# A two-block transformer kernel on one core: its prologue rearranged (scale rows first, shift rows last, squares added by GpSimd)

## The chip, the cores and the metric

One core of a Trainium2 chip runs the whole program. The metric is the device time of one execution in microseconds. Engine names are those of the profile: PE is TensorE's matmul, PEld its weight load, DVE VectorE, ACT ScalarE, POOL GpSimd, SP SyncE, whose queue issues the DMAs.

## The reference, cut to what matters

Two transformer-like blocks work on 1024 tokens of 1024 features in float32. The change touches only the start of the first one, up to its first gated products:

```
m = silu(c) @ a_mod_w + a_mod_b           # c is one row; m = shift, scale, gate
h = rmsnorm(x, a_norm_g) * (1 + scale) + shift
b_gate, c_gate, u, z = split(h @ a_w_in, 4)
y = b_gate * causal_dwconv(c_gate * u, a_conv_w) * silu(z)
```

`rmsnorm` divides every token by the root of the mean of its squares. This factor is one number for a token, so that `h @ w` equals `(x * g * (1 + scale)) @ w`, multiplied by the token's factor, plus `shift @ w`. The kernel uses this for the first two products: it starts them before the sum of squares is known.

## The kernel before, in words

Activations lie transposed: a feature tile is [128 features x 1024 tokens], and X is eight such tiles (k = 0 to 7). A product of one "chunk" gives 128 output features: eight steps (one for each k), each of six matmuls of 512 columns, because every operand is split in a high and a low part (HH and HL for activations, WH and WL for weights) and three of the four cross products are kept (`mm3`, L843; `step`, L851). A chunk's result stands in a pair of PSUM banks (PAIR[0] to PAIR[3]). ACT writes the high part of the weights (WH) from the loaded row WR, and POOL the low part (WL = WR - WH, L2747), each for a 128x1024 tile. With PAIR[0] and PAIR[1] and two slots each for WH and WL, chunks normally take turns.

The prologue before the change runs as follows.

- **SP** (L558 to L577) issues the DMAs in this order: the row c, the vectors (VEC), the weights of chunks 0 and 1, the four pieces of X (two tiles, 1 MB each) with two small constants behind the first piece, then for k = 0 to 7 the shift row and the scale row of `a_mod_w` (MRAW, 512 KB each), then the weights of chunks 2, 3 and 4, each behind a wait.
- **Squares**: ACT squares the eight tiles of X into XSQ (L1455), DVE adds them in pairs (L2133), and PE sums the four pairs over the partitions with a matrix of ones (L908).
- **Modulation**: `modulation` (L2115) multiplies a row tile with silu(c) and sums along it, which gives 128 values of shift or scale; it is called a dot below. `shift_and_scale(k)` (L2138) makes two dots and two operations of one column: the shift goes to MOD, the coefficient g * (1 + scale) to COEF.
- **Raw phase**: for each k, ACT writes HH = X * COEF (L1463), DVE writes HL = X * COEF - HH (`raw_low`, L2148), and PE makes the step k of chunks 0 and 1 (`input_chunks`, L914). Ahead of each step pair PE multiplies the split weights of the two chunks with the shift column of k (four matmuls of one column, L924), which gives the term `shift @ w` of chunks 0 and 1.
- **Fill**: `root` (L1427) makes the tokens' factors on ACT (Ln, then Exp). Then for each k DVE writes X * COEF * factor (L2050), ACT adds the shift and rounds it to HH (L1438), and DVE writes the low part HL (`fill_lo`, L2066; L2084). PE makes chunks 2 and 3 with these operands (`two_chunks`, L872), chunk 3 lagging one step behind chunk 2 until five of its steps are done. At k = 2 of the fill, DVE reads the raw results of chunks 0 and 1 out of PSUM into AE (L2166). ACT makes WH of chunks 2 and 3 in the same two slots that chunks 0 and 1 used, so after these have ended.
- **After the fill**: DVE multiplies the gates, runs the convolution and the products (`input_products`, L2177), then the six dots of the next 48 modulation rows, and PE goes on with chunk 4 and the loop over j.

The order on each engine is written out by hand; semaphores with constant counts tie the engines together. The rest of the program (attention, the second block, the two feed-forward matrices) is the same in both kernels.

Of the kernel before, what the change touches and what calls it, by code (L numbers as in the profile page):

```python
# [25 lines left out]
P = 128  # L26
# [165 lines left out]
def block_kernel(nc, xt, cb, vecs, consts, mods, wst, out):  # L192
    with ExitStack() as ctx:
        def sem(name):
            return ctx.enter_context(nc.semaphore(name))
# [54 lines left out]
        XSQ = nc.alloc_sbuf_tensor_at("XSQ", [P, KT * S], F32, offset=HL_AT)  # L250
        WR1 = nc.alloc_sbuf_tensor_at("WR1", [P, D], F32, offset=HL_AT - 4 * S)
        AE = [nc.alloc_sbuf_tensor_at(f"AE{i}", [P, S], F32, offset=(SCR0 + 127) // 128 * 128 + 4 * S * (6 + i)) for i in range(2)]
        WR3 = nc.alloc_sbuf_tensor_at("WR3", [P, D], F32, offset=(SCR0 + 127) // 128 * 128 + 4 * S)
# [124 lines left out]
        def vec(name, i=0):  # L378
            return col(VEC, i + _V[name])
# [35 lines left out]
        ld_c = sem("ld_c")  # L415
        ld_cb = sem("ld_cb")
# [5 lines left out]
        sq_pair = sem("sq_pair")  # L422
# [26 lines left out]
        a_raw_read = sem("a_raw_read")  # L449
        a_shift = sem("a_shift")  # L450
# [94 lines left out]
        def _(sp):  # L545
            def load_w(c, at=None):
                sp.wait_ge(w_lo, c)
                sp.dma_start(WR0[:, :], row(wst, c if at is None else at)).then_inc(ld_w, 16)
# [11 lines left out]
            sp.dma_start(VEC[:, :], vecs).then_inc(ld_c, 16)  # L560
            sp.dma_start(WR0[:, :], wst[0]).then_inc(ld_w, 16)
            sp.dma_start(WR1[:, :], wst[1]).then_inc(ld_w1, 16)
            for g in range(4):
                sp.dma_start(X[:, 2 * g * S:2 * (g + 1) * S], xt[:, 2 * g * S:2 * (g + 1) * S]).then_inc(ld_x[g], 16)
                if g == 0:
                    sp.dma_start(IDF[:, :], consts[:, K_ID:K_ID + P]).then_inc(ld_c, 16)
                    sp.dma_start(TRF[:, :], consts[:, K_TRI:K_TRI + P]).then_inc(ld_c, 16)
# [274 lines left out]
        def _(pe):  # L842
# [62 lines left out]
            for k in range(0, KT, 2):  # L905
                pe.wait_ge(sq_pair, k // 2 + 1)
                for h in (0, HALF):
                    last = pe.matmul(PS[:, 2 * S + h:2 * S + h + HALF], ONES[:, :], kt(XSQ, k)[:, h:h + HALF],  # L908
                                     start=k == 0, stop=k == KT - 2)
                    last.then_inc(ss if h and k == KT - 2 else sq_added, 1)  # L910

            u = USED["ain"]

            def input_chunks(j, first=False):  # L914
                if first:
                    pe.wait_ge(free[0], u[0])
                    pe.wait_ge(free[1], u[1])
                    pe.wait_ge(w_hi, C_AIN + 2)
                    pe.wait_ge(w_lo, C_AIN + 2)
                    for k in range(KT):  # L920
                        pe.wait_ge(a_raw_lo, k + 1)
                        for m in range(2):
                            for half in (WH[m], WL[m]):
                                pe.matmul(PS[:, 3 * S + m * HALF:3 * S + m * HALF + 1], half[:, k * P:(k + 1) * P].bitcast(F32),  # L924
                                          col(MOD, k), start=k == 0 and half is WH[m], stop=k == KT - 1 and half is WL[m])
# [485 lines left out]
        def _(act):  # L1411
# [41 lines left out]
            for k in range(KT):  # L1453
                act.wait_ge(ld_x[k // 2], 16)
                ins = act.activation(kt(XSQ, k), kt(X, k), ACT.Square)  # L1455
                if k:
                    ins.then_inc(sq, 1)
            act.wait_ge(s_sc, 1)
            for k in range(KT):
# [4 lines left out]
                if k == 0:  # L1464
                    load_ln()
                    act.wait_ge(ss, 1)
                    root(T[0], PAIR[2], TP)

            def first_input(k):
                if k < KT - 1:  # L1470
                    act.wait_ge(a_raw_read, k + 1)
                if k == 2:
                    split_w(2, 0)
                if k == 3:
                    act.wait_ge(ld_w, 48)
                    act.wait_ge(chunk_done, 3)
                    act.activation(WH[1][:, :], WR3[:, :], ACT.Identity).then_inc(w_hi, 1)
                    for m in range(2):
                        ins = act.activation(SM[:, 12 + m:13 + m], PS[:, 3 * S + m * HALF:3 * S + m * HALF + 1], ACT.Identity)
                    ins.then_inc(a_shift, 1)  # L1480
                    act.wait_ge(a_shift, 1)
                    act.wait_ge(free[1], 2)
                    act.activation(AE[1][:, :], AE[1][:, :], ACT.Identity, bias=SM[:, 13:14]).then_inc(ain_cu, 1)

            fill_hi("a", 0, before=first_input)
            act.wait_ge(ld_c, 48)
# [6 lines left out]
            def input_gates(j, first=False):  # L1493
# [5 lines left out]
                split_w(4 * j + 4, 0)  # L1499
# [6 lines left out]
                act.activation(T[2], PAIR[1], ACT.Sigmoid).then_inc(ain_sg, 1)  # L1506
# [506 lines left out]
            unit_hi(48, 0, 0)  # L2013
            unit_hi(48, 0, 1)
# [3 lines left out]
            unit_hi(48, 0, 2)  # L2018
            unit_hi(48, 0, 3)
            for i in range(5, 7):  # L2020
                down_weights_hi(0, 0, 0, i)
            unit_hi(48, 0, 4)
            hidden(UPS - 1, 1)
            unit_hi(48, 0, 5)
            unit_hi(48, 0, 6)
# [20 lines left out]
        def _(dve):  # L2046
# [77 lines left out]
            dve.wait_ge(ld_c, 48)  # L2124
# [6 lines left out]
            for k in range(0, KT, 2):  # L2131
                dve.wait_ge(sq, k + 1)
                dve.tensor_tensor(kt(XSQ, k), kt(XSQ, k), kt(XSQ, k + 1), ALU.add).then_inc(sq_pair, 1)  # L2133

# [3 lines left out]
            def shift_and_scale(k):  # L2138

                dve.wait_ge(ld_k[k], 32)  # L2140
                for dst, m in ((col(MOD, k), k), (col(COEF, k), KT + k)):
                    modulation(dst, MRAW[:, m * D:(m + 1) * D])
                dve.wait_ge(mod_done, 2 * k + 2)
                dve.tensor_tensor(col(MOD, k), col(MOD, k), vec("mod_b", k), ALU.add)
# [10 lines left out]
            shift_and_scale(0)  # L2155
            dve.wait_ge(ss, 1)
            for k in range(1, KT):
                shift_and_scale(k)
                raw_low(k - 1)
            raw_low(KT - 1)  # L2160

            def first_input(k):
                if k == 2:
# [13 lines left out]
            def input_products(j, first=False):  # L2177
# [4 lines left out]
                if first:  # L2182
                    dve.wait_ge(a_shift, 1)
# [14 lines left out]
                dve.tensor_tensor(T[3], PAIR[0], T[3], ALU.mult).then_inc(free[0], 1)  # L2198
# [5 lines left out]
                dve.tensor_tensor(T[2], PAIR[1], T[2], ALU.mult).then_inc(free[1], 1)  # L2204
# [538 lines left out]
        def _(pool):  # L2743
# [9 lines left out]
            split_w(2, 0)  # L2753
            pool.wait_ge(w_hi, 4)
            pool.tensor_tensor(WL[1][:, :], WR3[:, :], WH[1][:, :].bitcast(F32), ALU.subtract).then_inc(w_lo, 1)
# [221 lines left out]
```

## Time and profile before

| | us |
|---|---|
| median of 3 runs | 2800.58 (2798.49 to 2803.13) |
| span of the profiled execution | 2802.3 |
| PE busy | 2707.3 (97%) |
| DVE busy | 1614.1 (58%) |
| ACT busy | 1189.8 (42%) |
| POOL busy | 1109.0 (40%) |

The time of the profiled execution is its span, 2802.3 us; no other time was recorded for it. It lies within the three runs, 1.7 us above their median.

A row of the timeline gives the start in us from the span's start, the time in us, engine and line, what was written and read, how many instructions are merged (x2), and in brackets how long the engine had been idle before, and what ended that. A row of the stretches gives the stretch, its length, then for each engine the busy time and the number of instructions. A row of the chain gives start, us and what the time is put down to. Two records are written for each matmul with float32 operands that are not split.

### The profile page before, as it was taken

The numbers are of one execution on the slowest core, as the hardware profiler recorded it, in microseconds if no ns is written. First come the engines' busy times: TensorE is split into PE (matmuls) and PEld (weight loads), VectorE is DVE, ScalarE is ACT, GpSimd is POOL, SyncE is SP. The second block draws the span as 40 slices with busy tenths as digits, with TensorE's granted clock in tenths as the row PEclk, the third lists the DMA queues.
The fourth block names the chain that finished last, engine by engine and source line by source line (L and its number), as shares of the span: only waits on it lengthen the run. The fifth ranks groups of instructions, "written<-read, shape, count | busy, mean of one in ns | idle before, by whom it ended". The sixth has DMA issues, their size and how long they took to land.

```text
span 2802.3 us, 38646 instructions
## 1 busy us (share of the span) xinstructions
PE 2707.3 (97%) x13208; PEld 2150.3 (77%) x13208; DVE 1614.1 (58%) x2120; ACT 1189.8 (42%) x1779; POOL 1109.0 (40%) x753
## 2 busy tenths in 40 slices
PE   6999999999999998999999999999999999989998
PEld 4788888787777776878886777777788888868886
DVE  7744443304676776583015555554436766788888
ACT  4211123323555555442236667765434433334442
POOL 1222222121555554212221111211123988858886
PEclk9999999999999999999999999999999999999999
DMA  5333321344211213113330101101443343374442
GB/s 228 128 127 120 120 98 45 103 146 140 76 54 45 82 52 114 59 38 111 121 108 31 38 32 37 38 30 61 150 158 120 128 161 141 136 259 158 159 161 92
DMA packets 102110, 294.74 MB, mean 105 GB/s; under 512 B 9856, under 2 KB 10496, under 8 KB 101504
## 3 DMA queue, kind: packets, MB, share of 16 engines
q1 hardware_dynamic: 102016, 293.56, 29.7%
q8 instruction: 50, 0.82, 0.1%
q14 instruction: 44, 0.36, 0.0%
HBM read 220.12 MB, written 73.40 MB: 105 GB/s over the span
## 4 chain that ended last, share of the span: by engine, by line
PE 60%; issue 25%; POOL 6%; DVE 4%; ACT 3%; DMA 1%; POOLq 0%; SPq 0%; ACTq 0%; DVEq 0%
PE PS L847 27%; PE PS L1331 10%; PE PS L1383 5%; PE PS L1077 5%; POOL WL L2747 3%; PE PS L1049 2%; PE PS L982 2%; PE PS L1011 2%; PE PS L1026 2%; PE PS L1235 2%; POOL dL L2860 1%; PE PS L1216 1%; DVE dM L2679 1%; DVE bC L2296 1%; PE PS L1175 1%
## 5 line engine op out<-in xcount | busy, mean ns | idle before, releaser
L2747 POOL TENSOR_TENSOR WL<-WR,WH 128x1024 fp32r<-128x1024 f32 x147 | 367.7, 2501 | 1359.9 <-ACT WH L1421 1252.6
L847 PE MATMUL PS<-HH,WH 128*128 128x512 f32 x1712 | 546.0, 400 | 19.4 <-POOL WL L2747 5.9
L847 PE MATMUL PS<-HL,WH 128*128 128x512 f32 x1712 | 531.6, 392 | 0.0
L847 PE MATMUL PS<-HH,WL 128*128 128x512 f32 x1712 | 530.0, 391 | 0.0
L847 PEld LDWEIGHTS PS<-HH,WH 128*128 128x128 f32 x1712 | 315.4, 189 | 95.9 <-issue 26.3
L847 PEld LDWEIGHTS PS<-HL,WH 128*128 128x128 f32 x1712 | 323.4, 189 | 69.3
L847 PEld LDWEIGHTS PS<-HH,WL 128*128 128x128 f32 x1712 | 323.2, 189 | 69.3
L1421 ACT ACTIVATE WH<-WR 128x1024 fp32r<-128x1024 f32 x147 | 155.6, 1059 | 324.1 <-PE PS L847 226.6
L2771 POOL TENSOR_TENSOR bB<-bB,bC 128x256 f32<-128x256 f32 (+7 forms) x128 | 191.2, 1504 | 191.1 <-DVE bC L2296 191.1
L2296 DVE TENSOR_TENSOR_SCAN bC<-bN,EPSC 128x256 f32<-128x256 f32 (+7 forms) x128 | 222.7, 1751 | 57.3 <-ACT bN L1607 52.4
L2679 DVE TENSOR_TENSOR dM<-PS,dM 128x512 f32<-128x512 f32 x212 | 136.2, 678 | 1.6 <-PE PS L1383 1.2
L1607 ACT ACTIVATE bN<-PS 128x256 f32<-128x256 f32 (+7 forms) x128 | 84.6, 661 | 115.4 <-PE PS L1031 113.8
L2860 POOL TENSOR_TENSOR dL<-dRAW,dH 128x256 fp32r<-128x256 f32 x96 | 111.2, 1181 | 30.2 <-ACT dH L1984 30.2
L1984 ACT ACTIVATE dH<-dLF 128x256 fp32r<-128x256 f32 x128 | 50.5, 415 | 163.4 <-DVE dLF L2609 117.9
L2860 POOL TENSOR_TENSOR dL<-dLF,dH 128x256 fp32r<-128x256 f32 x128 | 103.1, 824 | 14.5 <-ACT dH L1984 14.5
L1077 PE MATMUL PS<-HH,WH 128*128 128x512 f32 x240 | 101.0, 421 | 7.6 <-DVE bQL L2057 6.8
L2437 DVE CUSTOM_DVE_ANT_0 dP<-PS,dBIAS 128x256 f32<-128x256 f32 (+7 forms) x128 | 91.7, 754 | 18.4 <-issue 17.0
L1910 ACT ACTIVATE uH<-uLF 128x512 fp32r<-128x512 f32 x64 | 40.5, 633 | 143.8 <-POOL uLF L2828 143.7
L2477 DVE RECIPROCAL SM<-SM 128x1 f32<-128x1 f32 x64 | 10.3, 162 | 155.3 <-ACT dP L1814 155.3
L2820 POOL TENSOR_TENSOR uL<-uLF,uH 128x512 fp32r<-128x512 f32 x64 | 98.5, 1548 | 3.2 <-ACT uH L1910 3.2
L1077 PE MATMUL PS<-HL,WH 128*128 128x512 f32 x240 | 98.4, 410 | 0.0
L1077 PE MATMUL PS<-HH,WL 128*128 128x512 f32 x240 | 97.2, 405 | 0.0
(348 smaller groups left out, 5618.7 us busy)
## 6 DMA issues: line engine op xcount, KB each, us to landing
WR<-wst SPq DMA_DIRECT2D x149, 512.0 KB, 3.4
uRAW<-wst SPq DMA_DIRECT2D x32, 512.0 KB, 4.8
hid<-uT SPq DMA_DIRECT2D x32, 512.0 KB, 2.8
dRAW<-wst SPq DMA_DIRECT2D x64, 256.0 KB, 3.6
HLF<-hid SPq DMA_DIRECT2D x28, 512.0 KB, 8.9
GLF<-hid SPq DMA_DIRECT2D x28, 512.0 KB, 8.1
TMP<-mods SPq DMA_DIRECT2D x24, 512.0 KB, 4.2
MR<-mods SPq DMA_DIRECT2D x24, 512.0 KB, 5.3
```

Of the source, the lines that this page charges most:

```text
L847: last = pe.matmul(PS[:, dst0 + q:dst0 + q + HALF], l, rr[:, k * S + q:k * S + q + HALF], start=a, stop=z)
L1077: last = pe.matmul(PS[:, 0:HALF], l[1 - ci][:, kb * P:(kb + 1) * P], rr[:, kb * S + c0:kb * S + c0 + HALF], start=i == 0, stop=i == 3 * KT ...
L1331: last = pe.matmul(up_bank(i), l[i][:, w], right(i, kp, low), start=kp == 0 and n == 0, stop=kp == 3 and n == 2)
L1383: last = pe.matmul(up_bank(i), l[i][:, w], right(i, kp + 2 * e, low), start=kp == 0 and n == 0, stop=kp == 1 and n == 2)
L1421: act.activation(WH[slot][:, :], WR0[:, :], ACT.Identity).then_inc(w_hi, 1)
L2296: dve.tensor_tensor_scan(bC[h][:, S - n:S][:, ::-1], c, EPSC[:, 0:1].broadcast_to([P, n]), 1.0, ALU.mult, ALU.bypass).then_inc(b_l[h], 1)
L2437: return dve.tensor_tensor_reduce(out=dst, in0=src, in1=bias, scale=-1.0, scalar=3.0e38, op0=ALU.add, op1=ALU.min, accum_out=least)
L2679: ins = dve.tensor_tensor(DM[m][i][:, :], up_bank(i), DM[m][i][:, :], ALU.add)
L2747: pool.tensor_tensor(WL[slot][:, :], WR0[:, :], WH[slot][:, :].bitcast(F32), ALU.subtract).then_inc(w_lo, 1)
L2771: pool.tensor_tensor(b, b, bC[h][:, S - n + 1:S + 1], ALU.mult).then_inc(b_a, 1)
L2820: pool.tensor_tensor(by_blocks(UL[i]), by_blocks(ULF[i]) if src is None else src, by_blocks(UH[i]).bitcast(F32), ALU.subtract).then_inc(up ...
L2860: pool.tensor_tensor(by_blocks(DL[i]), by_blocks(DLF[i]) if src is None else src, by_blocks(DH[i]).bitcast(F32), ALU.subtract).then_inc(up ...
```

## The change

- SP issues the first two weight rows before VEC, and behind each piece of X the two scale rows that belong to it. The weights of chunk 2 are issued ahead of piece 2, those of chunk 3 ahead of piece 3, and the eight shift rows come after all of these. A second, unsplit copy of chunk 0's weights (WA0) and the two constants follow, then the weights of chunk 4.
- ACT interleaves: two squares, then two high parts of the raw phase, and so on. The squares go to three buffers instead of XSQ. It writes WH of chunks 2 and 3 during the raw phase, into slots of their own (WH[2], WH[3]), which lie where scale rows were.
- POOL adds the squares: seven additions of 128x1024 into one accumulator, between the low parts of the weights of chunks 1 and 2. PE then sums a single tile over the partitions, ahead of step 7 of the raw phase.
- DVE makes one dot for each k in the raw phase (the scale row). The eight shift dots move into the fill: three ahead of k = 0, then one ahead of each of k = 1 to 5. The reading of chunks 0 and 1 out of PSUM moves from k = 2 to k = 3.
- PE drops the one-column matmuls from the raw phase and makes 24 of them in one go (8 for chunk 0 with the unsplit weights, 16 for chunk 1), after chunk 2 and five steps of chunk 3, and then the last three steps of chunk 3. Chunks 2 and 3 use PAIR[2] and PAIR[3].
- ACT splits the weights of chunk 4 at k = 3 of the fill instead of after it.

The core of the diff:

```diff
@@ sync
+            sp.dma_start(VEC[:, :], vecs).then_inc(ld_v, 16)
             for g in range(4):
+                if g == 2:
+                    sp.wait_ge(ld_w, 16)
+                    load_w(2, wait=1)
+                if g == 3:
+                    sp.wait_ge(ld_w1, 16)
+                    sp.wait_ge(mod_done, 2)
+                    sp.dma_start(WR3[:, :], wst[3]).then_inc(ld_w1, 16)
                 sp.dma_start(X[:, 2 * g * S:2 * (g + 1) * S], xt[:, 2 * g * S:2 * (g + 1) * S]).then_inc(ld_x[g], 16)
+                for k in (2 * g, 2 * g + 1):
+                    sp.dma_start(MRAW[:, (KT + k) * D:(KT + k + 1) * D], mods[KT + k]).then_inc(ld_k[k], 16)
             for k in range(KT):
-                for m in (k, KT + k):
-                    sp.dma_start(MRAW[:, m * D:(m + 1) * D], mods[m]).then_inc(ld_k[k], 16)
+                if k % 2 == 0:
+                    sp.wait_ge(ld_x[k // 2], 16)
+                sp.dma_start(MRAW[:, k * D:(k + 1) * D], mods[k]).then_inc(ld_x[k // 2], 16)
             sp.wait_ge(ld_w, 32)
+            sp.dma_start(WA0[:, :], wst[0]).then_inc(ld_w, 16)
@@ tensor
-            for k in range(0, KT, 2):
-                pe.wait_ge(sq_pair, k // 2 + 1)
...
                     for k in range(KT):
                         pe.wait_ge(a_raw_lo, k + 1)
-                        for m in range(2):
-                            for half in (WH[m], WL[m]):
...
+                        if k == KT - 1:
+                            sum_squares(KT - 1, T[0])
                         step(C_AIN, 0, 0, HH, HL, k)
                         step(C_AIN + 1, 1, 1, HH, HL, k, read=a_raw_read)
-                    two_chunks(C_AIN + 2, (0, 1), (0, 1), (u[0] + 1, u[1] + 1), (f_lo, FILL["a"]))
+                    pe.wait_ge(rs, 1)
+                    for k in range(KT):
+                        pe.wait_ge(f_lo, FILL["a"] + k + 1)
+                        step(C_AIN + 2, 2, 2, HH, HL, k)
+                        if 1 <= k <= 5:
+                            step(C_AIN + 3, 3, 3, HH, HL, k - 1)
+                    pe.wait_ge(free[0], u[0] + 1)
+                    pe.wait_ge(ld_w, 48)
+                    for m, parts in enumerate(((WA0[:, :],), (WH[1][:, :].bitcast(F32), WL[1][:, :].bitcast(F32)))):
+                        for k in range(KT):
+                            for part in parts:
+                                last = pe.matmul(PS[:, m * HALF:m * HALF + 1], part[:, k * P:(k + 1) * P], col(MOD, k),
+                                                 start=k == 0 and part is parts[0], stop=k == KT - 1 and part is parts[-1])
+                    last.then_inc(a_shift, 1)
+                    for k in range(5, KT):
+                        step(C_AIN + 3, 3, 3, HH, HL, k)
@@ scalar
+            for k in range(0, KT, 2):
+                first_square(k)
+                first_square(k + 1)
+                raw_hi_a(k)
+                raw_hi_a(k + 1)
+                if k == 4:
+                    act.wait_ge(ld_w, 32)
+                    act.activation(WH[2][:, :], WR0[:, :], ACT.Identity).then_inc(w_hi, 1)
+            act.wait_ge(ld_w1, 32)
+            act.activation(WH[3][:, :], WR3[:, :], ACT.Identity).then_inc(w_hi, 1)
+            load_ln()
+            act.wait_ge(ss, 1)
+            root(T[0], PAIR[2], TP)
@@ vector
+            def shift_row(k):
+                dve.wait_ge(ld_x[k // 2], 48)
+                modulation(col(MOD, k), MRAW[:, k * D:(k + 1) * D])
+                dve.wait_ge(mod_done, KT + k + 1)
+                dve.tensor_tensor(col(MOD, k), col(MOD, k), vec("mod_b", k), ALU.add).then_inc(a_bias, 1)
+                dve.wait_ge(a_bias, k + 1)
...
             def first_input(k):
-                if k == 2:
+                for n in ((0, 1, 2), (3,), (4,), (5,), (6,), (7,))[k] if k < 6 else ():
+                    shift_row(n)
+                if k == 3:
                     for m in range(2):
                         dve.wait_ge(chunk_done, C_AIN + m + 2)
@@ gpsimd
-            split_w(2, 0)
+            for k in range(1, KT):
+                pool.wait_ge(sq, k)
+                if k > 1:
+                    pool.wait_ge(sq_added, k - 1)
+                pool.tensor_tensor(T[0], T[0], T[2 + k % 2], ALU.add).then_inc(sq_added, 1)
+            split_w(2, 2)
             pool.wait_ge(w_hi, 4)
-            pool.tensor_tensor(WL[1][:, :], WR3[:, :], WH[1][:, :].bitcast(F32), ALU.subtract).then_inc(w_lo, 1)
+            pool.tensor_tensor(WL[3][:, :], WR3[:, :], WH[3][:, :].bitcast(F32), ALU.subtract).then_inc(w_lo, 1)
```

## Rows read from the trace of the kernel before

**Rows 1.** Busy time by stretch: PE, PEld, DVE, ACT, POOL, then PE clock, DMA

```profile
45.00:50.00 5.00, 5.00 (x30) 4.30 (x28) 4.96 (x10) 1.15 (x1) 0.00 (x0) 1.00 0.00 0
...
65.00:70.00 5.00, 2.71 (x11) 1.95 (x12) 4.93 (x4) 3.49 (x6) 2.53 (x1) 1.00 0.16 64
```

**Rows 2.** Chain that ended last, from 28 us on: start, us, what

```profile
29.94 5.12 PE PS L847 x12
...
42.39 0.79 PE PS L924 x8
43.18 2.89 PE PS L847 x12
```

**Rows 3.** Timeline of PE

```profile
21.39 1.98 PE L908 MATMUL PS<-XSQ,ONES 128*128 128x512 f32 x4 [0.39 <-DVE XSQ L2133]
...
63.12 0.70 PE L847 MATMUL PS<-HH,WH 128*128 128x512 f32 x2 [2.37 <-POOL WL L2747]
...
88.28 0.70 PE L847 MATMUL PS<-HH,WH 128*128 128x512 f32 x2
...
123.33 1.11 PE L847 MATMUL PS<-HH,WH 128*128 128x512 f32 x2 [2.12 <-DVE TMP L2190]
```

**Rows 4.** Timeline of DVE, raw phase

```profile
21.45 1.23 DVE L2117 CUSTOM_DVE_ANT_0 MRAW<-MRAW,TMP 128x1024 f32<-128x1024 f32 x1
...
46.66 1.28 DVE L2152 SCALAR_TENSOR_TENSOR HL<-X,COEF,HH 128x1024 fp32r<-128x1024 f32 x1
...
50.47 2.66 DVE L2152 SCALAR_TENSOR_TENSOR HL<-X,COEF,HH 128x1024 fp32r<-128x1024 f32 x2
```

**Rows 5.** Timeline of DVE, fill

```profile
69.91 1.28 DVE L2050 SCALAR_TENSOR_TENSOR TMP<-X,COEF,TMP 128x1024 f32<-128x1024 f32 x1
...
72.43 1.28 DVE L2050 SCALAR_TENSOR_TENSOR TMP<-X,COEF,TMP 128x1024 f32<-128x1024 f32 x1
...
78.67 2.59 DVE L2084 SCALAR_TENSOR_TENSOR HL<-TMP,MOD,HH 128x1024 fp32r<-128x1024 f32 x2
```

**Rows 6.** Timeline of ACT

```profile
10.25 2.00 ACT L1455 ACTIVATE XSQ<-X 128x1024 f32<-128x1024 f32 x2 [1.51 <-DMA X<-xt]
...
18.07 2.00 ACT L1455 ACTIVATE XSQ<-X 128x1024 f32<-128x1024 f32 x2 [0.49 <-DMA X<-xt]
...
26.82 1.10 ACT L1429 ACTIVATE TMP<-PS,EPSC 128x1024 f32<-128x1024 f32 x1
...
29.23 1.06 ACT L1430 ACTIVATE TMP<-TMP 128x1024 f32<-128x1024 f32 x1
```

**Rows 7.** Timeline of POOL

```profile
9.79 2.35 POOL L2751 TENSOR_TENSOR WL<-WR,WH 128x1024 fp32r<-128x1024 f32 x1
60.64 2.34 POOL L2747 TENSOR_TENSOR WL<-WR,WH 128x1024 fp32r<-128x1024 f32 x1 [48.49 <-ACT WH L1421]
...
92.64 2.40 POOL L2747 TENSOR_TENSOR WL<-WR,WH 128x1024 fp32r<-128x1024 f32 x1 [4.50 <-ACT WH L1421]
101.54 2.39 POOL L2747 TENSOR_TENSOR WL<-WR,WH 128x1024 fp32r<-128x1024 f32 x1 [6.50 <-ACT WH L1421]
...
127.87 2.65 POOL L2747 TENSOR_TENSOR WL<-WR,WH 128x1024 fp32r<-128x1024 f32 x1 [13.91 <-ACT WH L1421]
```

**Rows 8.** Timeline of DVE, instructions that run while POOL works

```profile
11.10 1.06 DVE L2129 TENSOR_TENSOR GFE<-VEC 128x8 f32<-128x8 f32 x1
...
60.80 1.22 DVE L2166 TENSOR_TENSOR AE<-PS,TMP 128x1024 f32<-128x1024 f32 x1 [0.16 <-PE PS L847]
...
101.54 3.46 DVE L2117 CUSTOM_DVE_ANT_0 MR<-MR,TMP 128x1024 f32<-128x1024 f32 x1 [0.40 <-DMA MR<-mods]
...
128.19 3.40 DVE L2117 CUSTOM_DVE_ANT_0 MR<-MR,TMP 128x1024 f32<-128x1024 f32 x1
```

**Rows 9.** Timeline of DVE, first dot after the fill

```profile
99.91 1.23 DVE L2117 CUSTOM_DVE_ANT_0 TMP<-TMP,TMP 128x1024 f32<-128x1024 f32 x1 [3.80 <-DMA TMP<-mods]
```

**Rows 10.** Busy time by stretch, columns as in rows 1

```profile
120.00:140.00 20.00, 17.88 (x73) 14.33 (x72) 16.12 (x18) 3.04 (x3) 4.42 (x2) 0.91 0.50 158
```

More of the change, by code:

```diff
@@ L249, in block_kernel @@
         MR = [T[0], nc.alloc_sbuf_tensor_at("MR1", [P, D], F32, offset=(SCR0 + 127) // 128 * 128 + 4 * S * 7)[:, :]]
-        XSQ = nc.alloc_sbuf_tensor_at("XSQ", [P, KT * S], F32, offset=HL_AT)
         WR1 = nc.alloc_sbuf_tensor_at("WR1", [P, D], F32, offset=HL_AT - 4 * S)
-        AE = [nc.alloc_sbuf_tensor_at(f"AE{i}", [P, S], F32, offset=(SCR0 + 127) // 128 * 128 + 4 * S * (6 + i)) for i in range(2)]
-        WR3 = nc.alloc_sbuf_tensor_at("WR3", [P, D], F32, offset=(SCR0 + 127) // 128 * 128 + 4 * S)
+        AE = [nc.alloc_sbuf_tensor_at(f"AE{i}", [P, S], F32, offset=(SCR0 + 127) // 128 * 128 + 4 * S * (14 + i)) for i in range(2)]
+        WA0, WR3 = (nc.alloc_sbuf_tensor_at(n, [P, D], F32, offset=(SCR0 + 127) // 128 * 128 + 4 * S * (8 + i))
+                    for i, n in enumerate(("WA0", "WR3")))
+        for i in range(2):
+            for slots, n in ((WH, "WH"), (WL, "WL")):
+                slots.append(nc.alloc_sbuf_tensor_at(f"{n}{2 + i}", [P, D], F32R,
+                                                     offset=(SCR0 + 127) // 128 * 128 + 4 * S * (10 + 2 * i + (n == "WL"))))
         GH = place("GH", KT * S, F32R)
@@ L545, in _, with load_w @@
         def _(sp):
-            def load_w(c, at=None):
-                sp.wait_ge(w_lo, c)
+            def load_w(c, at=None, wait=None):
+                sp.wait_ge(w_lo, c if wait is None else wait)
                 sp.dma_start(WR0[:, :], row(wst, c if at is None else at)).then_inc(ld_w, 16)
@@ L903, in _ @@
             pe.wait_ge(s_const, 1)
-            for k in range(0, KT, 2):
-                pe.wait_ge(sq_pair, k // 2 + 1)
[L907 to L910, printed above, removed]
             u = USED["ain"]
@@ L1452, in _, with first_square, raw_hi_a @@
             act.activation(WH[1][:, :], WR1[:, :], ACT.Identity).then_inc(w_hi, 1)
-            for k in range(KT):
+            def first_square(k):
                 act.wait_ge(ld_x[k // 2], 16)
-                ins = act.activation(kt(XSQ, k), kt(X, k), ACT.Square)
+                if k >= 3:
+                    act.wait_ge(sq_added, k - 2)
+                ins = act.activation(T[2 + k % 2] if k else T[0], kt(X, k), ACT.Square)
                 if k:
                     ins.then_inc(sq, 1)
-            act.wait_ge(s_sc, 1)
-            for k in range(KT):
+            def raw_hi_a(k):
                 act.wait_ge(a_coef, k + 1)
@@ L1471, in first_input @@
                     act.wait_ge(a_raw_read, k + 1)
-                if k == 2:
-                    split_w(2, 0)
                 if k == 3:
-                    act.wait_ge(ld_w, 48)
+                    act.wait_ge(ld_w, 64)
                     act.wait_ge(chunk_done, 3)
[L1477 to L1483, printed above, removed]
-            fill_hi("a", 0, before=first_input)
-            act.wait_ge(ld_c, 48)
+                    act.activation(WH[0][:, :], WR0[:, :], ACT.Identity).then_inc(w_hi, 1)
+            fill_hi("a", 0, before=first_input)
+            act.wait_ge(a_shift, 1)
+            for m in range(2):
+                ins = act.activation(SM[:, 12 + m:13 + m], PS[:, m * HALF:m * HALF + 1], ACT.Identity)
+            ins.then_inc(free[0], 1)
+            act.wait_ge(free[0], 3)
+            act.wait_ge(free[1], 2)
+            act.activation(AE[1][:, :], AE[1][:, :], ACT.Identity, bias=SM[:, 13:14]).then_inc(ain_cu, 1)
+            act.wait_ge(ld_c, 32)
             act.activation(IDR[:, :], IDF[:, :], ACT.Identity)
@@ L1505, in input_gates @@
                     act.wait_ge(free[1], 2 * j + 2)
-                act.activation(T[2], PAIR[1], ACT.Sigmoid).then_inc(ain_sg, 1)
+                act.activation(T[2], PAIR[3 if first else 1], ACT.Sigmoid).then_inc(ain_sg, 1)
                 split_w(4 * j + 5, 1)
@@ L2017, in _ @@
             hidden(UPS - 1, 0)
-            unit_hi(48, 0, 2)
-            unit_hi(48, 0, 3)
+            unit_hi(32, 0, 2)
+            unit_hi(32, 0, 3)
             for i in range(5, 7):
                 down_weights_hi(0, 0, 0, i)
-            unit_hi(48, 0, 4)
+            unit_hi(32, 0, 4)
             hidden(UPS - 1, 1)
-            unit_hi(48, 0, 5)
-            unit_hi(48, 0, 6)
+            unit_hi(32, 0, 5)
+            unit_hi(32, 0, 6)
             def down_pass(t, half, loads, e, last=False):
@@ L2036, in down_pass @@
                             unit_hi(loads, 1 - e, i)
-            down_pass(0, 0, 64, 0)
+            down_pass(0, 0, 48, 0)
             with act.Fori(0, DOWNS // PASS // 2 - 1) as i:
-                down_pass(2 * PASS * i + PASS, 4 * i + 2, 32 * i + 80, 1)
-                down_pass(2 * PASS * i + 2 * PASS, 4 * i + 4, 32 * i + 96, 0)
-            down_pass(DOWNS - PASS, (DOWNS - PASS) // 2, 16 * (DOWNS // PASS + 3), 1, last=True)
+                down_pass(2 * PASS * i + PASS, 4 * i + 2, 32 * i + 64, 1)
+                down_pass(2 * PASS * i + 2 * PASS, 4 * i + 4, 32 * i + 80, 0)
+            down_pass(DOWNS - PASS, (DOWNS - PASS) // 2, 16 * (DOWNS // PASS + 2), 1, last=True)
         @block.vector
@@ L2130, in _, with scale_row @@
             dve.tensor_scalar(GFE[:, :], GFE[:, :], EPS, None, ALU.add).then_inc(gfe, 1)
-            for k in range(0, KT, 2):
-                dve.wait_ge(sq, k + 1)
-                dve.tensor_tensor(kt(XSQ, k), kt(XSQ, k), kt(XSQ, k + 1), ALU.add).then_inc(sq_pair, 1)
             scale_b = MOD[:, KT:2 * KT]
             links(dve.tensor_scalar(scale_b, VEC[:, _V["mod_b"] + KT:_V["mod_b"] + 2 * KT], 1.0, None, ALU.add))
[L2138 to L2144, printed above, removed]
+            def scale_row(k):
+                dve.wait_ge(ld_k[k], 16)
+                modulation(col(COEF, k), MRAW[:, (KT + k) * D:(KT + k + 1) * D])
+                dve.wait_ge(mod_done, k + 1)
                 dve.scalar_tensor_tensor(out=col(COEF, k), in0=col(COEF, k), scalar=col(MOD, KT + k),
                                          in1=vec("a_g", k), op0=ALU.add, op1=ALU.mult).then_inc(a_coef, 1)
+            def shift_row(k):
[4 more added lines that the diff above has]
+                dve.wait_ge(a_bias, k + 1)
             def raw_low(k):
@@ L2197, in input_products @@
                 dve.wait_ge(chunk_done, 4 * j + 4)
-                dve.tensor_tensor(T[3], PAIR[0], T[3], ALU.mult).then_inc(free[0], 1)
+                if first:
+                    dve.tensor_tensor(T[3], PAIR[2], T[3], ALU.mult).then_inc(a_bias, 1)
+                    dve.wait_ge(a_bias, KT + 1)
+                else:
+                    dve.tensor_tensor(T[3], PAIR[0], T[3], ALU.mult).then_inc(free[0], 1)
                 if not first:
@@ L2203, in input_products @@
                 dve.wait_ge(ain_sg, j + 1)
-                dve.tensor_tensor(T[2], PAIR[1], T[2], ALU.mult).then_inc(free[1], 1)
+                dve.tensor_tensor(T[2], PAIR[3 if first else 1], T[2], ALU.mult).then_inc(free[1], 1)
                 dve.wait_ge(free[0], 2 * j + 3)
```

39 lines of the change are left out of this document (11 added, 28 removed).

## The prediction

> **What bounds the kernel now.** The page comes first: PE is busy 97% of the span, so a time can only be won where PE stands still or runs slowly, and the change touches the first 100 us. The stretches of the first 140 us [rows 1, 10] show DVE busy throughout (4.96 of 5 us at 45 us, 4.93 at 65 us) while POOL does next to nothing. The chain of waits [rows 2] shows a raw phase in which PE needs 0.79 + 2.89 = 3.68 us for one k, and the timeline of DVE [rows 4] a period of 50.47 - 46.66 = 3.81 us for the same k: two dots, two small operations, one low part. So DVE sets the pace there. In the fill DVE needs 72.43 - 69.91 = 2.52 us for a k [rows 5], PE about 2.8 for two steps, and what PE loses there are waits for weights made by POOL (2.37 us at 63.12 [rows 3]). I measure the prologue by one mark, the start of chunk 4: 88.28 us [rows 3]. After it PE stands still once, for 2.12 us at 123.33, behind DVE [rows 3], and its clock drops behind that stall: a mean of 0.91 over 20 us [rows 10] is 0.09 * 20 = 1.8 us more. The rest follows PE and stays as it is.
>
> **Do DVE and POOL work side by side?** That decides this change, since it gives POOL seven additions of 128x1024 in the middle of DVE's busiest time. The two timelines laid beside each other [rows 7, 8] say no. A product of 128x8 on DVE, a thing of eight columns, starts at 11.10 and takes 1.06, nearly as long as a dot over 1024: it ends at 12.16, when POOL's subtraction (9.79 + 2.35 = 12.14) does. The dot at 101.54 takes 3.46 instead of 1.23 us while POOL works from 101.54 to 103.93. At 127.87 it is POOL that waits first (2.65 instead of 2.34), for the dot ahead, and then it goes between two dots of DVE: the next takes 3.40 (128.19 to 131.59; POOL ends at 130.52). So each runs alone, for a whole instruction, and POOL gets its turn even when DVE has more to do. One pair does overlap: at 60.80 DVE takes its usual 1.22 us while POOL works from 60.64, and there DVE reads one operand from PSUM.
>
> The Trainium skill (SBUF — State Buffer, Who interferes with whom) has this as an exclusive lock for the whole instruction, between a GpSimd instruction that reads SBUF and a VectorE instruction with two SBUF inputs; by that rule, the trace agrees. It also spares instructions with one SBUF input: if the low part of chunk 4's weights fell beside the two readings out of PSUM, the sum below would be 2.3 us smaller. The same skill (Perfetto Trace Analysis) warns that moving work from one of these two engines to the other might not help.
>
> **The change, part by part.**
>
> 1. *Start of the dots.* Now the first dot starts at 21.45 [rows 4], behind the pair sums of the squares. ACT's first square starts with the landing of piece 0 at 10.25, the last piece lands at 18.07 [rows 6], so 1 MB takes (18.07 - 10.25) / 3 = 2.6 us. The first scale row lands 1.3 us behind piece 0, at 11.6; POOL ends its second subtraction at 12.14. The first dot starts at about 12.1, 9.4 us sooner.
>
> 2. *DVE's own work from the first dot to the last low part of the fill.* It is moved, not shortened: 8 * 3.81 = 30.5 for the dots and raw low parts, 8 * 2.52 = 20.2 for the fill, 1.3 for its last low part, 2 * 1.22 = 2.4 for the two readings [rows 4, 5, 8]. Sum 54.4 us. The pair additions that it loses lay ahead of the first dot. Each shift row adds a wait for its own result, not shown before: between 0 and 0.2 us, I take 0.
>
> 3. *POOL's work inside that stretch.* Seven additions (not shown before; nearest is the subtraction of the same size, 2.34 [rows 7]), and the low parts of the weights of chunks 2, 3 and 4, which now fall into the raw phase and the fill. Ten instructions of 2.34 are 23.4 us. All of DVE's instructions there but the two readings have two operands in SBUF, the one-column ones too, as the 128x8 product shows. Ends: 0, if nothing is excluded, and 23.4. Would they fall into pauses of DVE? The rows arrive faster than DVE with POOL can take them: 8 MB from piece 0 to the last scale row are 20.9 us, to 31.1 us, while 8 dots, 8 low parts and 7 additions alone need 8 * 2.6 + 16.4 = 37. I take 23.4.
>
> 4. *The tokens' factors.* The sum over the partitions (1.98 us [rows 3]) and the root (30.29 - 26.82 = 3.5 [rows 6]) now follow the last raw low part. DVE makes three shift dots meanwhile (3 * 1.4 = 4.2). Left: 5.5 - 4.2, say 1.1 to 1.3; I take 1.2.
>
> Last low part of the fill: 12.1 + 54.4 + 23.4 + 1.2 = 91.1 us. Now it is 78.67 + 2.59 = 81.26 [rows 5].
>
> 5. *PE behind it.* Now 88.28 - 81.26 = 7.0 us are left, all backlog. After: chunk 2's last step 1.4 (half of 2.89 [rows 2]), 24 one-column matmuls in one go (four take 0.79, so 4.7), three steps of chunk 3 at 1.4, together 10.3. Chunk 4 starts at 101.4, 13.1 later. The eight one-column matmuls saved, the earlier start of PE, and the weights of chunks 2 and 3 that no longer wait (2.37 at 63.12) save nothing, since DVE comes last: in the raw phase a k takes DVE over 4.5 us, PE under 3, or 5.12 at half clock [rows 2].
>
> 6. *Behind chunk 4's start.* SP issues the weights of chunk 6 and then the next rows of modulation once POOL has made chunk 5's low part. Now that is 92.64 + 2.40 = 95.04, 6.8 us behind the mark. After, chunk 4's weights are ready long before, the new weights of chunk 5 are loaded at the end of the fill, and ACT splits them behind the sigmoid: 1.1 + 1.1 + 2.4 = 4.6 us behind the mark. DVE waited 3.80 us for these rows [rows 9], so its string of dots comes about 2.2 us sooner relative to PE, and the stall of 2.12 with its 1.8 of slow clock should go. Ends: 0 and 3.9; I take 3.9, since 2.2 just covers it and a collision with POOL (the 3.46 at 101.54) may fall away too.
>
> SP itself: the added waits for chunks 0's and 1's weights and for the second dot hold the queue at about 9.8 and 17 us, and each time the issued transfers last until 17.9 and 24.3. Behind the second wait stand chunk 3's weights, piece 3, two scale rows and all shift rows; nobody misses them. Cost 0; if that cover were gone, some 2 us. The constants' conversions on ACT lie under chunk 3.
>
> **Sum.** 13.1 - 3.9 = +9.2 us. Against the profiled execution 2802.3 + 9.2 = 2811.5; the median of the runs is 1.7 lower: 2809.8, rounded to 2810.
>
> **Rivals.**
>
> - *Nothing is excluded, the fill comes sooner* (faster). Decides where POOL's additions meet DVE's dots, between 12 and 50 us. Raw low parts then follow the DMA: last scale row at 31.1, a dot and two low parts more, with some backlog 36. Fill 23.9, eight shift dots 8 * 1.3 = 10.4, 2 us of waiting for the root: 72.3; PE's 10.3 more: 82.6, 5.7 sooner than now. With 3.9 it gives -9.6: 2791. For it: only the 1.22 beside POOL at 60.80. Against: the three rows at 11.10, 101.54 and 128.19. 12%.
> - *Excluded, but partly hidden* (no change). Some 3 us of POOL fall into DVE's waits for rows, ACT or the root, and chunk 4's low part lies beside the readings (2.3): +3.9, 2804.5. For it: ACT and DVE do wait for each other in the new order. 22%.
> - *More is lost.* The stall at 123.33 stays in another place (3.9 not gained), and PE's clock halves during the 4.7 us of one-column matmuls (up to 1.8, as behind the stall [rows 10]): +14.9, 2815. For it: the two chains are only 0.1 apart. 16%.
>
> **Numbers.** The forecast itself, 2805 to 2813, has 50%. The range takes in the second and third rival and leaves out the first: 2797 to 2818. What a measurement can tell from no change is about 0.2%, 5.6 us. Slower by more: 50 + 16 = 66%, of which I give 2 to "same" as the forecast's lower edge: 64%. Within: 22 + 2 = 24%. Faster: 12%.
>
> **What the new profile would show.** First dot near 12 us; POOL with seven additions of 2.3 us or more between 13 and 45; dots or small column operations of DVE with 2 to 3.5 us beside them, and instructions of 1.3 beside none; last low part of the raw phase near 50 (36 if nothing is excluded); last low part of the fill near 91; 4.7 us of L924-like matmuls, three steps, chunk 4 at about 101; no stall near 135. Wrong would be the forecast if dots keep 1.22 us while POOL adds, or if PE shows long waits for anything but DVE's low parts in the fill.

## The result, and the profile after

The changed kernel takes 2811.91 us in the median of 5 runs (2809.70 to 2814.99), the kernel before 2800.58 (2798.32 to 2803.13, 5 runs): a ratio of 1.0044, with a 95% interval of 1.0033 to 1.0055. It is slower by 11.3 us. The forecast was 2810, with a range of 2797 to 2818.

| mark, us | before | predicted | after |
|---|---|---|---|
| first dot starts | 21.45 | 12.1 | 11.57 |
| last raw low part ends | 53.13 | near 50 | 51.25 |
| last low part of the fill ends | 81.26 | 91.1 | 90.24 |
| chunk 4 starts | 88.28 | 101.4 | 106.54 |
| later stall of 2.12 us | yes | gone | gone |
| span | 2802.3 | | 2809.9 |

The timelines of DVE and POOL in the raw phase, for two of the eight k, answer to [rows 4, 7, 8]:

```profile
11.57 1.23 DVE L2144 CUSTOM_DVE_ANT_0 MRAW<-MRAW,TMP 128x1024 f32<-128x1024 f32 x1
12.72 0.08 DVE L2144 DVE_READ_ACCUMULATOR2_ANT COEF<- 128x1 f32 x1
12.84 2.17 DVE L2166 SCALAR_TENSOR_TENSOR COEF<-COEF,MOD,VEC 128x1 f32<-128x1 f32 x1
...
20.93 1.27 DVE L2181 SCALAR_TENSOR_TENSOR HL<-X,COEF,HH 128x1024 fp32r<-128x1024 f32 x1
22.12 3.40 DVE L2144 CUSTOM_DVE_ANT_0 MRAW<-MRAW,TMP 128x1024 f32<-128x1024 f32 x1
25.46 0.08 DVE L2144 DVE_READ_ACCUMULATOR2_ANT COEF<- 128x1 f32 x1
25.57 0.22 DVE L2166 SCALAR_TENSOR_TENSOR COEF<-COEF,MOD,VEC 128x1 f32<-128x1 f32 x1
...
44.49 6.76 DVE L2181 SCALAR_TENSOR_TENSOR HL<-X,COEF,HH 128x1024 fp32r<-128x1024 f32 x2
```

```profile
11.87 3.12 POOL L2790 TENSOR_TENSOR TMP<-TMP,TMP 128x1024 f32<-128x1024 f32 x1 [0.44 <-ACT TMP L1473]
18.61 5.83 POOL L2790 TENSOR_TENSOR TMP<-TMP,TMP 128x1024 f32<-128x1024 f32 x2 [3.62 <-ACT TMP L1473]
28.00 5.86 POOL L2790 TENSOR_TENSOR TMP<-TMP,TMP 128x1024 f32<-128x1024 f32 x2 [3.56 <-ACT TMP L1473]
38.38 6.18 POOL L2790 TENSOR_TENSOR TMP<-TMP,TMP 128x1024 f32<-128x1024 f32 x2 [4.51 <-ACT TMP L1473]
44.52 2.35 POOL L2780 TENSOR_TENSOR WL<-WR,WH 128x1024 fp32r<-128x1024 f32 x1
46.84 3.34 POOL L2793 TENSOR_TENSOR WL<-WR,WH 128x1024 fp32r<-128x1024 f32 x1
```

Read them together: the coefficient of one column, 0.22 us at 25.57, takes 2.17 at 12.84 and ends at 15.01, when POOL's first addition does (11.87 + 3.12 = 14.99). POOL's own 3.12 hold 0.8 us of waiting for the dot of 11.57. The dot at 22.12 takes 3.40. The two last raw low parts take 6.76 where two took 2.66 [rows 4], beside POOL's low parts of the weights of chunks 2 and 3. Over the whole phase four coefficients and three dots, one beside each addition, take 14.5 us more than alone: 2.1 us for each addition. DVE starts 9.9 us sooner than before and ends the phase only 1.9 us sooner, with eight dots still to make that the kernel before had behind it.

The timeline of PE behind the fill, which has no counterpart among the rows of before but the four matmuls of one column in [rows 2]:

```profile
92.25 1.84 PE L939 MATMUL PS<-MOD,WA 128*128 128x1 f32 x16
93.95 0.36 PE L939 MATMUL PS<-MOD,WH 128*128 128x1 f32 x2
94.18 0.36 PE L939 MATMUL PS<-MOD,WL 128*128 128x1 f32 x2
94.40 0.48 PE L939 MATMUL PS<-MOD,WH 128*128 128x1 f32 x2
94.74 0.57 PE L939 MATMUL PS<-MOD,WL 128*128 128x1 f32 x2
...
99.86 0.57 PE L939 MATMUL PS<-MOD,WL 128*128 128x1 f32 x2
100.28 1.20 PE L856 MATMUL PS<-HH,WH 128*128 128x512 f32 x2
...
104.70 0.65 PE L856 MATMUL PS<-HH,WL 128*128 128x512 f32 x2
...
106.54 0.62 PE L856 MATMUL PS<-HH,WH 128*128 128x512 f32 x2
```

And two stretches (columns as in [rows 1]), the second answering to [rows 10]:

```profile
94.00:106.00 12.00, 12.00 (x49) 10.84 (x50) 3.92 (x4) 4.08 (x10) 0.00 (x0) 0.57 0.01 2
...
120.00:140.00 20.00, 20.00 (x90) 16.57 (x89) 14.60 (x17) 1.06 (x1) 4.97 (x2) 1.00 0.71 229
```

PE is busy without a gap from 94 to 106, yet its granted clock there is 0.57 of full speed: it falls to the lower of its two levels (1.2 GHz) when PE has made one-column matmuls for 2.5 us. The run of 24 takes 8.03 us (92.25 to 100.28), where it was priced at 4.7, and the three steps behind it 6.26 instead of 4.2. The stall of [rows 3] at 123.33 is gone: PE is busy 20.00 of 20 us at full clock, and it has no wait at all from chunk 4's start to 411 us. POOL ends chunk 5's low part at 111.19, 4.65 us behind the start of chunk 4 (forecast 4.6, before 6.8), and SP issues the next modulation row at 111.60, 5.06 behind; before it was 95.44, 7.16 behind.

### The profile page after: what moved, and what is told of

It reads as the page before. It is cut to its first block, busy times and chain, and to the rows that moved or that the text cites. A ratio compares the mean times of both kernels' runs of the same rounds, so it can differ in the third digit from the quotient of the medians.

```text
span 2809.9 us, 38612 instructions
## 1 busy us (share of the span) xinstructions
PE 2704.9 (96%) x13180; PEld 2153.5 (77%) x13180; DVE 1630.4 (58%) x2116; ACT 1189.8 (42%) x1779; POOL 1128.0 (40%) x760
## 4 chain that ended last, share of the span: by engine, by line
PE 65%; issue 22%; DVE 5%; POOL 4%; ACT 3%; DMA 0%; POOLq 0%; SPq 0%; ACTq 0%; DVEq 0%
PE PS L856 29%; PE PS L1346 10%; PE PS L1398 8%; PE PS L1092 5%; POOL WL L2780 3%; PE PS L1064 2%; PE PS L997 2%; PE PS L1026 2%; PE PS L1041 2%; PE PS L1250 2%; PE PS L1231 1%; DVE dM L2712 1%; DVE bC L2329 1%; PE PS L1190 1%; DVE dM L2753 1%
```

## The experiments

All but the last three start from the changed kernel. "Mark" is the start of chunk 4. The ratios are to runs of the kernel before that were taken with each group: its median was 2799.86 us for e1 to e4, 2800.03 for e5 to e8 and 2801.83 for e9 to e11.

**e1: additions of one column.** The sum of squares is left out but for tile 0 and one column.

```diff
-pool.tensor_tensor(T[0], T[0], T[2 + k % 2], ALU.add).then_inc(sq_added, 1)
+pool.tensor_tensor(T[0][:, 0:1], T[0][:, 0:1], T[2 + k % 2][:, 0:1], ALU.add).then_inc(sq_added, 1)
```

> The changed kernel, but POOL's seven additions of the squares take one column instead of 1024 (the sum of squares is left out but for tile 0 and those columns). Everything else, DVE's instructions included, stays. If POOL and DVE exclude each other, seven times 2.3 us = 16 us vanish from DVE's path: the last raw low part ends near 35 instead of 51.2, the last low part of the fill near 75 instead of 90.2, the time falls by 13 to 16 us to about 2797. If the additions run beside DVE at no cost (the new order or the tail is what costs), both ends stay and the time is 2812.

Measured 2799.61 us, ratio to before 1.0001 (0.9992 to 1.0010). The ends of the two phases in its timeline of DVE:

```profile
34.80 2.65 DVE L2181 SCALAR_TENSOR_TENSOR HL<-X,COEF,HH 128x1024 fp32r<-128x1024 f32 x2
...
73.18 2.59 DVE L2111 SCALAR_TENSOR_TENSOR HL<-TMP,MOD,HH 128x1024 fp32r<-128x1024 f32 x2
```

The last raw low part ends at 37.45 instead of 51.25, the last one of the fill at 75.77 instead of 90.24, 14.5 us sooner; the mark comes at 90.45. Of the 16.1 us at the mark 2.3 are not the additions' doing: the same run of 24 one-column matmuls takes 5.75 us here (77.77 to 83.52) and not 8.03, since the clock falls later in it. Seven additions cost 12 us of the whole time, and what is left of the change is worth nothing against before.

**e2: the additions on DVE.**

```diff
-            for k in range(1, KT):
-                pool.wait_ge(sq, k)
...
-                pool.tensor_tensor(T[0], T[0], T[2 + k % 2], ALU.add).then_inc(sq_added, 1)
...
+                dve.tensor_tensor(T[0], T[0], T[2 + k % 2], ALU.add).then_inc(sq_added, 1)
```

> The changed kernel with the seven additions made by DVE, one behind each raw low part, instead of by POOL. If POOL and DVE exclude each other, seven times 2.34 us of POOL are exchanged for seven times 1.2 us of DVE on the same path: 8 us less, the last low part of the fill near 82, the time near 2804. If POOL works beside DVE for nothing, DVE has 8 us more to do and the time is near 2820. The sign tells the two apart.

Measured 2806.69 us, ratio 1.0021 (1.0012 to 1.0031). Last low part of the fill at 81.42, mark at 98.02, 8.5 us sooner than in the changed kernel. DVE has more to do and is sooner done. Counted from e1, which has no whole additions, the seven cost 14.5 us at the end of the fill when POOL makes them (90.24 against 75.77) and 5.7 us when DVE does (81.42 against 75.77).

**e3 and e4: where the one-column matmuls stand.** In e3, six behind each of the steps k = 3 to 6 of the fill; in e4, still behind the fill, in groups of 6, 9 and 9, each ahead of one of the last three steps.

```diff
+                        for kk in {3: (0, 1), 4: (2, 3), 5: (4, 5), 6: (6, 7)}.get(k, ()):
+                            for m, parts in enumerate(((WA0[:, :],), (WH[1][:, :].bitcast(F32), WL[1][:, :].bitcast(F32)))):
+                                for part in parts:
+                                    last = pe.matmul(PS[:, m * HALF:m * HALF + 1], part[:, kk * P:(kk + 1) * P], col(MOD, kk),
...
```

```diff
                     for k in range(5, KT):
+                        for kk in ((0, 1), (2, 3, 4), (5, 6, 7))[k - 5]:
...
                         step(C_AIN + 3, 3, 3, HH, HL, k)
```

> The changed kernel with the 24 one-column matmuls no longer in one go behind the fill: six of them behind each of PE's steps k = 3 to 6 of the fill, where PE waits for DVE. If the long run of one-column matmuls is what halves the clock and stands behind DVE's last low part (8.0 us from 92.25 to 100.28, then three steps in 6.3 instead of 4.2), chunk 4 starts near 98 instead of 106.5 and the time falls by 8 us, to about 2804. If the clock falls for another reason (the low load in the fill), only the 4.7 us of column work at full clock go: about 2807.

> The changed kernel with the 24 one-column matmuls still behind the fill, but in three groups (6, 9 and 9), each followed by one of the last three steps of chunk 3. The work is the same and nothing more is hidden. If the long run is what halves the clock, the groups of 1.2 and 1.8 us keep it full: chunk 4 starts 5.4 us sooner (8.0 + 6.3 against 4.7 + 4.2), time about 2806.5. If the clock falls whatever the grouping, nothing changes: 2812.

Marks 101.95 and 101.93, both 4.6 us sooner. Times 2811.72 (1.0037, 1.0023 to 1.0050) and 2812.98 (1.0049, 1.0035 to 1.0063): no gain. A piece of e3's timeline of PE:

```profile
88.30 0.28 PE L940 MATMUL PS<-MOD,WA 128*128 128x1 f32 x2
...
89.33 0.36 PE L940 MATMUL PS<-MOD,WL 128*128 128x1 f32 x2
89.56 0.72 PE L856 MATMUL PS<-HH,WH 128*128 128x512 f32 x2
90.11 0.63 PE L856 MATMUL PS<-HL,WH 128*128 128x512 f32 x2
```

Six one-column matmuls take 1.26 us, and the steps behind them run at full clock. In e4 the granted clock is 1.00 from 90 to 102 us. That both marks agree shows what the 4.6 us were: not hidden work (e4 hides nothing), but the clock. The other runs say the same: the clock falls within the 24 one-column matmuls in all five other kernels that keep them in one go (e1, e2, e5, e6, e7, 3.0 to 4.9 us behind their start), and does not fall in those that spread them (e3, e8 to e11). e3 hides nothing either, against what was expected: from 76 us on PE carries a backlog, so that what is put between its steps lies on the path. In e4 the last one-column matmul comes later relative to chunk 4, and with it DVE's work behind it (it starts 0.2 us behind the mark, in the changed kernel 4.6 ahead of it), and the stall of before is back:

```profile
136.86 0.70 PE L856 MATMUL PS<-HH,WH 128*128 128x512 f32 x2 [2.11 <-DVE TMP L2221]
```

**e5 and e6: what POOL does beside DVE.** The sum of squares is left out in both.

```diff
+pool.memset(T[0], 1.0).then_inc(sq_added, 1)
```

```diff
+pool.tensor_scalar(T[0], T[2 + k % 2], 1.0, None, ALU.mult).then_inc(sq_added, 1)
```

> The changed kernel, with each of POOL's seven additions replaced by a memset of the same 128x1024 accumulator (the sum of squares is left out). POOL is as often at work between DVE's instructions, but reads nothing. If any POOL instruction of that size shuts DVE out, DVE's dots and coefficients beside them still take 2 to 3.4 us and the last raw low part ends near 51. If it is POOL's reading of SBUF that shuts DVE out (the rule of the Trainium skill's page SBUF — State Buffer), they take 1.2 and 0.2 us as alone and the last raw low part ends near 37, as with the one-column additions.

> The changed kernel, with each of POOL's seven additions replaced by a multiplication of one tile by a constant (one operand instead of two; the sum of squares is left out). If one operand read from SBUF is enough to shut DVE out, each costs DVE as much as POOL takes for it, so the last raw low part ends between 37 and 51, by seven times the new duration. If two operands are needed, it ends near 37.

One execution each: 2798.92 and 2799.98 us. The last raw low part ends at 37.40 and 37.45, as with the one-column additions. A memset takes 0.95 us (two in 2.02), and DVE's coefficients and dots beside the memsets take 0.22 and 1.22 us. The Trainium skill (SBUF — State Buffer, Who interferes with whom) says that a GpSimd instruction which only writes does not contend; the trace agrees. The multiplication by a constant was not as either expectation had it. POOL:

```profile
12.04 3.53 POOL L2790 TENSOR_SCALAR TMP<-TMP 128x1024 f32<-128x1024 f32 x1 [0.46 <-ACT TMP L1473]
```

and DVE beside it:

```profile
12.98 0.86 DVE L2166 SCALAR_TENSOR_TENSOR COEF<-COEF,MOD,VEC 128x1 f32<-128x1 f32 x1
13.77 1.21 DVE L2144 CUSTOM_DVE_ANT_0 MRAW<-MRAW,TMP 128x1024 f32<-128x1024 f32 x1
15.16 1.28 DVE L2181 SCALAR_TENSOR_TENSOR HL<-X,COEF,HH 128x1024 fp32r<-128x1024 f32 x1
```

POOL works from 12.04 to 15.57; DVE loses 0.64 us at the start (0.86 for 0.22) and then takes its usual 1.21. Beside each of the seven it is much the same: one DVE instruction takes 0.6 to 0.8 us more, 4.7 us in all. So a POOL instruction with one operand from SBUF delays DVE, but does not shut it out to its end, and the whole-instruction lock that the prediction names is not what this run shows. That the raw phase still ends with that of e1 and e5 is a coincidence: those two wait 2.6 us for rows in it and lose 2.0 us to chunk 2's low part, which in e6 comes behind it. e6's fill ends at 77.21, 1.4 us behind e1's.

**e7 and e8: PE sums the squared tiles, no additions.** e8 has e3's spreading too.

```diff
+                        for i in (k, k + 1) if k % 2 == 0 else ():
+                            pe.wait_ge(sq, max(i, 1))
+                            for h in (0, HALF):
+                                last = pe.matmul(PS[:, 2 * S + h:2 * S + h + HALF], ONES[:, :], T[(0, 2, 3)[i % 3]][:, h:h + HALF],
+                                                 start=i == 0, stop=i == KT - 1)
+                            last.then_inc(ss if i == KT - 1 else sq_added, 1)
```

> The changed kernel without any addition: PE sums all eight squared tiles over the partitions, two matmuls of 512 columns each, two tiles ahead of every second step of the raw phase. DVE loses 16 us of being shut out, PE gets 7 * 2.0 = 14 us more in a phase where it waits for DVE. Last low part of the fill near 80, then the run of one-column matmuls at half clock as in the changed kernel: chunk 4 near 96, time near 2802. If PE's 14 us stand on the path instead, the last low part of the fill comes near 88 and the time is near 2809.

> As e7, with the one-column matmuls spread behind PE's steps k = 3 to 6 of the fill. Chunk 4 between 87 and 92, where e7 has 96, no run at half clock; the time near 2795, faster than the kernel before. If PE is the bound through the fill, the spreading is worth only what the half clock cost (4.6 us in e3), and the time is near 2798.

e7: last low part of the fill at 79.51, mark at 96.23, 2805.04 us (1.0018, 1.0009 to 1.0027). e8: mark at 90.89, 2801.46 us (1.0008, 0.9999 to 1.0017). The marks are as expected. The times are not: e7 is 3 us above its 2802, e8 6.5 us above its 2795 and 3 above the 2798 of its other case. e8 wins back some 10 of the 11.3 us and leaves nothing out.

**e9 to e11: all shift dots ahead of the fill.** e9 and e11 start from e8, e10 from e2 with e3's spreading; e11 also splits chunk 4's weights at k = 7 instead of 3.

```diff
-                for n in ((0, 1, 2), (3,), (4,), (5,), (6,), (7,))[k] if k < 6 else ():
+                for n in range(KT) if k == 0 else ():
```

> As e8, with all eight shift dots ahead of the fill instead of three ahead and five between its steps. In e8 DVE waits 2.65 us for the tokens' factors ahead of the fill, and in the fill PE waits for DVE until 65 us and then carries a backlog to the end. With the dots out of the fill DVE feeds a step every 2.5 us: last low part of the fill near 76 instead of 79, PE nearly without waits from 53 on, chunk 4 near 83 where e8 has 90.9; the time 6 to 8 us below e8, near 2795. If later stages give it back, as the 4.6 us of e3 were, it stays near 2800.

> The other way to avoid POOL: DVE makes the seven additions (as e2), one-column matmuls spread (as e3), all shift dots ahead of the fill (as e9). DVE has 8 us more in the raw phase than e9, PE 14 us less. Last low part of the fill near 80, chunk 4 near 86; the time near 2797, 2 to 3 us above e9.

> As e9, with the split of chunk 4's weights moved from k = 3 to k = 7 of the fill, so that POOL's subtraction (2.3 us) meets DVE at the end of the fill instead of in it. If DVE still sets the pace there, chunk 4 comes up to 2 us sooner; if PE does, nothing changes within the 2 us that these kernels scatter by.

| | last low part of the fill | mark | us | ratio to before |
|---|---|---|---|---|
| e9 | 75.76 | 87.81 | 2798.65 | 0.9990 (0.9981 to 0.9999) |
| e10 | 79.64 | 91.68 | 2801.57 | 1.0001 (0.9992 to 1.0009) |
| e11 | 76.47 | 86.48 | 2797.10 | 0.9989 (0.9980 to 0.9998) |

DVE is where it was expected; PE is 5 us behind the expectation in e9 (87.8, not 83), for it still waits 6.83 us for the first low part of the fill and 2.21 for the third, and then has thirteen steps and the 24 one-column matmuls to make without a pause (64.43 to 87.81):

```profile
56.21 1.19 PE L856 MATMUL PS<-HH,WH 128*128 128x512 f32 x2 [6.83 <-issue]
64.43 0.74 PE L856 MATMUL PS<-HH,WH 128*128 128x512 f32 x2 [2.21 <-DVE HL L2117]
```

e11's chunk 4 comes 1.3 us sooner than e9's, although its fill ends 0.7 us later; in the times the two cannot be told apart. Both are 13 to 15 us faster than the changed kernel. Against the kernel before they are 3.2 and 4.7 us faster by the medians and about 3 by the ratios. The upper ends of their intervals are 0.9999 and 0.9998, the best two of ten such ratios, so a gain over the kernel before is likely but not shown.

## Why the prediction was right, point by point

- *POOL and DVE exclude each other* (the reading on which all hung): right. Shown by the changed kernel's rows and by e1 (12 us less when POOL's operands shrink and DVE's stay) and e2 (DVE doing the work itself is 8.5 us sooner at the mark). The rival at 12%, that nothing is excluded, had 72.3 for the last low part of the fill; e1, where only one column of the additions is left, has 75.77. What e6 adds is a limit to the reading: it holds where POOL reads two operands. And DVE waits for no row between 11.57 and 51.25, so that the cost of 0 for SP's added waits held here; with the additions gone (e1, e5) it waits 2.6 us for rows.
- *Steps 1 to 4*, the path of DVE: 91.1 forecast, 90.24 measured. The first dot came at 11.57 instead of 12.1. From there to the last low part of the fill it was 78.7 us, forecast at 54.4 + 23.4 + 1.2 = 79.0. Inside that two misses cancel. The wait for the tokens' factors was 3.05 us and not 1.2: PE was still busy with step 6 at half clock (48.01 to 53.29) when the last raw low part ended at 51.25, and the sum of squares came behind it. DVE also waits 0.39 us for its own result in the first shift row. And the ten POOL instructions cost DVE 20.8 us, 2.6 less than the 23.4 of the sum: 14.5 beside the additions, 4.1 in the two last raw low parts, 2.1 beside chunk 4's low part.
- *Step 5*, PE behind it: 10.3 us forecast, 16.3 measured (106.54 - 90.24). This is the term that was mis-sized. What PE still had to do of the steps ahead of the one-column matmuls took 2.0 us (92.25 - 90.24), where the sum had 1.4. The one-column matmuls in one go took 8.03 us instead of 4.7, and the three steps behind them 6.26 instead of 4.2. Together that is 0.6 + 3.3 + 2.1 = 6.0 us. The forecast had the fall of the clock only in the rival "more is lost", with at most 1.8 us. e4 shows that it is the uninterrupted run: the same matmuls in three groups give 4.6 us back at the mark.
- *Step 6*, the stall behind chunk 4's start: right, 3.9 us forecast, 4.1 measured. From the mark to the first matmul on GL in the next stage (397.5, 411.6 us) it is 309.2 us before and 305.1 after. The same 305.1 stand in e1, e2, e3 and e7 to e11; in e4, where a stall of 2.11 us is back, it is 307.5. Two stalls of one length thus cost 4.1 us and 2.4: behind the one before, the clock falls (0.66 from 123 to 128 us), behind the one in e4 it does not (1.00 from 136 to 142). No run shows why.
- *The sum*: +13.1 - 3.9 = +9.2 forecast. At 400 us the changed kernel is 14.1 behind, at the end of the two profiled executions 7.6, in the medians 11.3. So the forecast was 2 us short of the medians with an error of 6 us in one term, and that it came so near was luck: DVE's path was 0.9 us shorter than forecast, and 2.8 us of the 14.1 were won back behind 400 us, for which the forecast had no term. The direction and the path are not luck, the last 3 us are.

**What stays open** is the way from the mark to the end. e3 is 4.6 us ahead of the changed kernel at 400 us and ends with the same 2809.9 us span; e1, e7 and e8 lose 1 to 3 us, by the medians, of what they have at 400 us. In e3's trace PE enters the attention stage (699.4 us in the kernel before) at 707.9, the changed kernel at 710.9, and they reach the stage behind it (1315.3 in the kernel before) at 1324.1 and 1323.0, e3 now later. One piece can be named: from 480 to 520 us the granted clock is 0.91 in e3 and 0.96 in the changed kernel, 2 us. The granted clock falls to half for some microseconds at other moments in each trace. No run here shows what decides when, so it is left at this: what a kernel has gained or lost at 400 us arrives in its median only within 3 us, either way.

## What to carry to other kernels

Before giving GpSimd work "because it is idle", lay its timeline beside VectorE's and look for an instruction of a few columns that takes two microseconds: where both read two operands from SBUF, most of the time of one is lost to the other. An addition given away cost VectorE 2.1 us here, where making it itself takes 1.2. Matmuls of one column were cheap between full ones (six in 1.26 us) and dear in a run (24 in up to 8.03 us, and 2.1 us more on the steps behind). And a profile's mark near the change (here chunk 4's start) tells parts of a change apart that the total time, with its scatter of 3 us, cannot.

## What was not expected of the hardware

- The clock fell while PE was busy without a gap: 0.57 of full speed from 94 to 106 us, in a run of one-column matmuls. It fell 2.5 us behind the start of that run, in e1 4.9 us:

```profile
82.16 0.36 PE L939 MATMUL PS<-MOD,WH 128*128 128x1 f32 x2
82.38 0.42 PE L939 MATMUL PS<-MOD,WL 128*128 128x1 f32 x2
82.67 0.56 PE L939 MATMUL PS<-MOD,WH 128*128 128x1 f32 x2
```

  The Trainium skill (TensorE: Matmul & The Clock Gate, Part 1: The HAM clock gate) ties the clock to how busy the engine has been. In the profile's rows PE is busy 12.00 of these 12 us, so its busy time alone would not have foretold the fall.
- POOL's multiplication by a constant (one operand from SBUF) takes 2.8 to 3.5 us, longer than the 2.34 of a subtraction of two tiles, and delays DVE by only 0.6 to 0.8 us.
- An in-place addition of a constant on DVE, eight columns wide, took 2.28 us beside POOL's subtraction, where a multiplication by a constant of a single column took 0.15 at 7.57, also beside POOL (6.78 to 9.12). It kept DVE busy until the first dot at 11.57:

```profile
7.57 0.15 DVE L2153 TENSOR_SCALAR GS<-VEC 128x1 f32<-128x1 f32 x1
7.75 1.40 DVE L2156 TENSOR_TENSOR GFE<-VEC 128x8 f32<-128x8 f32 x1
9.18 2.28 DVE L2157 TENSOR_SCALAR GFE<-GFE 128x8 f32<-128x8 f32 x1
```

  In the kernel before, where POOL had ended at 12.14, the same instruction took 0.17 us:

```profile
12.20 0.17 DVE L2130 TENSOR_SCALAR GFE<-GFE 128x8 f32<-128x8 f32 x1
```
